# An encoder step: other score banks for the memory steps, input weight splits in parts, memory splits later

## The chip, the cores and the metric

The kernel runs on 1 core of one Trainium2 chip. The metric is the device time of one execution in microseconds (us). Its engines work side by side: TensorE (PE in the profile, with its weight loads as PEld), VectorE (DVE), ScalarE (ACT), GpSimd (POOL) and SyncE (SP), which here only issues transfers. Each runs its own instruction list in order and waits on semaphores that the others raise.

## The reference

One inference step of a one-layer streaming encoder, all in float32: 1024 prompt tokens and 8 x 16 sample tokens (9 tiles of 128 tokens), model width 1024. What matters here, shortened:

```python
qa, ka, va, qb, kb, vb = project(rmsnorm(hp, g_attn), w_in, pos_p)      # 1024 x 2304, rotary on q and k
oa = swa_prompt(qa, ka, va, a_sinks)                # windowed attention with sinks
ob = rmsnorm(diff_prompt(qb, kb, vb, lam), g_subln) * (1.0 - lam_init)  # (softmax1 - lam*softmax2) @ v, 4 heads
hp = hp + jnp.concatenate([oa, ob], axis=-1) @ w_out
mk, mv = mem_kv(mem_prompt, g_mem, w_xkv)           # memory keys and values: 256 x 1024 @ 1024 x 2048
hp = hp + cross_attn(rmsnorm(hp, g_cross), mk, mv, w_xq, w_xo)
hp = hp + sq_relu_mlp(rmsnorm(hp, g_mlp), w_up, w_down)
y_prompt = rmsnorm(hp, g_final)
# the same for the 8 sample streams, against their caches; new keys, values, windows are outputs too
```

## The kernel before

Every float32 product is made from three float32r products: an operand is split into a high part (a copy that rounds, on ScalarE) and a low part (the difference, on VectorE), and TensorE adds high x high, high x low and low x high in a PSUM bank. Weights come in units of 1024 x 256 values, 1 MB each: units 0 to 8 are `w_in`, 9 to 16 `w_xkv`, 17 to 20 `w_out`. A unit is loaded into one of two slots of `w_raw` (`load_next` on ScalarE's queue), `split_hi` copies 128 x 2048 values into `w_hi`, `split_lo` (L1403) subtracts them into `w_lo` in one instruction, L1406. `project` (L1867) makes one projection: 24 matmuls (8 slices of k times 3 products) of 256 columns, for one tile of tokens and one unit. Projections are numbered q. Each is evacuated by VectorE into `stage` (`finish_projection`, L1427; with rotary it is three or four instructions), and GpSimd issues the store.

First stage (to about 60 us): the nine tiles of x are squared (ScalarE), their root is taken (GpSimd), they are scaled (VectorE), transposed on TensorE (`turn`, L1845, 8 transposes a tile) and split (`turned_hi`, `turned_lo`), and unit 0 is projected. TensorE turns tile t + 1 ahead of projection t. VectorE's order for tile t is: scale tile t + 2, low part of tile t + 1, evacuate projection t. GpSimd takes the store of projection t - 2 before the root of tile t + 1.

Then units 1 and 2, and from 115 us on the attention, a software pipeline over the 84 entries of `STEPS`, of which steps 0 to 63 are one phase: steps 0 to 15 are heads 0 and 1 of the differential attention ("diff", t = 0 to 7 key tiles), 16 to 39 the windowed one ("swa", and "swas" for samples), 40 to 63 heads 2 and 3 with the eight samples ("diffs") between them. In step i TensorE issues: scores of i, a preparing transpose (`PREP`: keys, queries, head tiles, memory tiles), value product of i - 2, other transposes, a projection "beside" (`BESIDE`), transposes of the probabilities of i - 1. VectorE in step i: output copy of i - 3 (`out_dve`), maxima of i (`row_max`), sums and combination of i - 1 (`combine`), the low parts of prepared tiles, then `finish_beside` for the step's projections, each followed by `split_lo` of the next unit when q is the first of its unit. ScalarE in step i: transposed probabilities of i - 2, exponentials of i, copies of prepared tiles, and at a unit's first projection `unit_begun`: load of unit u + 2 and `split_hi` of unit u + 1.

`KV_BESIDE` lists, counted from step 40, the 16 steps that get a projection of the memory. PSUM has 8 banks: scores use 0 to 3, transposed probabilities 4 and 5, outputs 6, and bank 7 is shared by nearly all preparing transposes and, in steps 40 to 65, by all memory projections (`beside_bank`, L157). A projection on bank 7 waits for the copy of the last prepared tile there and a preparing transpose waits for the evacuation of the last projection. Scores of a "diff" step with t < 4 in heads 2 and 3 use two banks of one parity, with t >= 4 all four, those of "diffs" banks 0 and 1. Windowed scores use banks 0 and 1 in every step, so each waits for the exponentials of the step before.

The last memory projection is in step 65. When it has ended, SyncE loads three tiles of the residual, and the output projection, the cross attention and the MLP follow from about 632 us on.

## Time and profile before

| | us |
|---|---|
| three runs: median (lowest to highest) | 1876.59 (1875.58 to 1884.19) |
| the profiled execution | 1878.05 |
| its span, first to last instruction | 1876.2 |
| TensorE busy | 1757.1 (94%) |
| VectorE busy | 879.5 (47%) |
| ScalarE busy | 545.9 (29%) |
| GpSimd busy | 172.2 (9%) |

The chain of work that ended last is 84% TensorE, 6% VectorE, 3% ScalarE, 3% transfers. Times below are counted from the start of the span. In a timeline a row is start, duration, engine, line, operation, output <- inputs, shapes, count and, in brackets, how long the engine had idled and what ended that. TensorE's times depend on the clock that was granted; it has two levels, 1.2 and 2.4 GHz, and a granted clock of 1.00 is the upper one.

### The profile page before, as it was taken

Reading aid. Unit: us, or ns where it says so; the run is one execution under the profiler, and the core shown is the slowest. Engines: PE = TensorE matmul, PEld = TensorE weight load, DVE = VectorE, ACT = ScalarE, POOL = GpSimd, SP = SyncE. Lnnn points to the kernel's source line nnn. Section 1 sums busy time; section 2 is a strip of 40 time slices with the busy share of each in tenths; the row PEclk is TensorE's granted clock in tenths of the full one; section 3 lists DMA queues with packets and bytes.
Section 4 is the critical chain, followed back from the end, with each engine's and each line's share of the span. In section 5 each row is a group of like instructions: output and inputs, shape, how many; then the busy total and the mean of one; then the engine's idle time right before and its main releaser. Section 6 shows DMA issues by size and latency. Waiting matters only on the chain.

```text
span 1876.2 us, 29420 instructions
## 1 busy us (share of the span) xinstructions
PE 1757.1 (94%) x11905; PEld 1623.3 (87%) x11905; DVE 879.5 (47%) x1683; ACT 545.9 (29%) x1192; POOL 172.2 (9%) x355
## 2 busy tenths in 40 slices
PE   5998989987797799998999999999999999999997
PEld 5998889876676799997889999999999999999996
DVE  4557555655445425323432554444444444444445
ACT  4213343565444214104520421111111111111112
POOL 2113321112112101110000100000000000000002
PEclk9999999989998899999999999999999999999998
DMA  6312322245453620726451011111111111101102
GB/s 206 108 63 65 105 65 81 66 148 162 165 183 111 240 75 16 263 96 231 171 180 46 23 47 44 45 45 45 45 45 45 45 45 45 36 31 45 56 0 101
DMA packets 107484, 170.39 MB, mean 91 GB/s; under 512 B 7497, under 2 KB 75721, under 8 KB 107369
## 3 DMA queue, kind: packets, MB, share of 16 engines
q1 hardware_dynamic: 79464, 126.78, 20.0%
q0 software_dynamic: 8160, 22.29, 3.5%
q10 hardware_dynamic: 19760, 19.92, 3.3%
q8 instruction: 71, 1.16, 0.3%
q14 instruction: 29, 0.23, 0.0%
HBM read 138.17 MB, written 31.72 MB: 91 GB/s over the span
## 4 chain that ended last, share of the span: by engine, by line
PE 84%; DVE 6%; DMA 3%; ACT 3%; issue 3%; POOL 1%; SPq 0%; ACTq 0%; DVEq 0%; POOLq 0%
PE banks L1922 27%; PE banks L1875 24%; PE banks L2303 21%; PE banks L2012 2%; DMA w_raw<-in_cache_mem_k 1%; DVE w_lo L1406 1%; PE banks L2069 1%; PE banks L1863 1%; PE banks L2171 1%; PE banks L2191 1%; PE banks L2160 1%; PE banks L2099 1%; PE banks L2139 1%; ACT probs L1236 1%; PE banks L2049 1%
## 5 line engine op out<-in xcount | busy, mean ns | idle before, releaser
L1875 PE MATMUL banks<-w_hi,xt_hi 128*128 128x256 f32 x1224 | 355.3, 290 | 13.6 <-DVE xt_lo L1420 3.0
L1875 PE MATMUL banks<-w_lo,xt_hi 128*128 128x256 f32 x1224 | 344.5, 281 | 0.0
L1875 PE MATMUL banks<-w_hi,xt_lo 128*128 128x256 f32 x1224 | 344.4, 281 | 0.0
L1922 PE MATMUL banks<-xt_hi,w_hi 128*128 128x384 f32 x960 | 323.0, 336 | 0.0
L1922 PE MATMUL banks<-xt_hi,w_lo 128*128 128x384 f32 x960 | 322.7, 336 | 0.0
L1922 PE MATMUL banks<-xt_lo,w_hi 128*128 128x384 f32 x960 | 322.6, 336 | 0.0
L1875 PEld LDWEIGHTS banks<-w_hi,xt_hi 128*128 128x128 f32 x1224 | 233.1, 190 | 21.4 <-issue 9.2
L1070 ACT ACTIVATE w_hi<-w_raw 128x2048 fp32r<-128x2048 f32 x61 | 116.8, 1916 | 418.9 <-PE banks L2303 225.8
L1799 DVE TENSOR_TENSOR h<-h,banks 128x512 f32<-128x512 f32 x288 | 192.2, 685 | 98.7 <-PE banks L2303 96.7
L1875 PEld LDWEIGHTS banks<-w_lo,xt_hi 128*128 128x128 f32 x1224 | 233.2, 191 | 0.0
L1875 PEld LDWEIGHTS banks<-w_hi,xt_lo 128*128 128x128 f32 x1224 | 232.9, 190 | 0.0
L2303 PE MATMUL banks<-w_hi,hid_hi 128*128 128x512 f32 x576 | 224.9, 390 | 0.0
L2303 PE MATMUL banks<-w_hi,hid_lo 128*128 128x512 f32 x576 | 224.6, 390 | 0.0
L2303 PE MATMUL banks<-w_lo,hid_hi 128*128 128x512 f32 x576 | 224.0, 389 | 0.0
L1779 DVE TENSOR_TENSOR sq<-sq 128x384 f32<-128x384 f32 x96 | 49.3, 555 | 305.9 <-ACT hid_hi L1355 305.9
L1922 PEld LDWEIGHTS banks<-xt_lo,w_hi 128*128 128x128 f32 x960 | 180.5, 188 | 1.4
L1922 PEld LDWEIGHTS banks<-xt_hi,w_hi 128*128 128x128 f32 x960 | 180.5, 188 | 1.2
L1922 PEld LDWEIGHTS banks<-xt_hi,w_lo 128*128 128x128 f32 x960 | 180.5, 188 | 0.0
L1352 ACT ACTIVATE sq<-banks 128x384 f32<-128x384 f32 x96 | 47.1, 492 | 389.8 <-PE banks L1922 389.7
L2303 PEld LDWEIGHTS banks<-w_hi,hid_lo 128*128 128x128 f32 x576 | 108.1, 188 | 23.4
L2303 PEld LDWEIGHTS banks<-w_lo,hid_hi 128*128 128x128 f32 x576 | 108.1, 188 | 21.5
L2303 PEld LDWEIGHTS banks<-w_hi,hid_hi 128*128 128x128 f32 x576 | 108.1, 188 | 21.2
(217 smaller groups left out, 2231.4 us busy)
## 6 DMA issues: line engine op xcount, KB each, us to landing
w_raw<-in_w_up SPq DMA_DIRECT2D x16, 1024.0 KB, 5.3
w_raw<-in_w_down SPq DMA_DIRECT2D x16, 1024.0 KB, 4.9
w_raw<-in_w_xkv ACTq DMA_DIRECT2D x8, 1024.0 KB, 7.1
kc_diff<-in_cache_diff_k SPq DMA_DIRECT2D x16, 512.0 KB, 3.9
vc_diff<-in_cache_diff_v SPq DMA_DIRECT2D x8, 1024.0 KB, 5.9
w_raw<-in_cache_mem_k SPq DMA_DIRECT2D x16, 512.0 KB, 8.0
w_raw<-in_w_in ACTq DMA_DIRECT2D x7, 1024.0 KB, 5.7
scaled<-mix_d SPq DMA_DIRECT2D x9, 512.0 KB, 5.6
```

The source lines that it names most:

```text
L1070: return nc.scalar.activation(out, in_, ACT.Copy, **kw)
L1236: last = nc.scalar.activation(p[:, g, :], s[:, g, :], ACT.Exp, bias=bias, accum_out=den[:, i % 4, c:c + 1])
L1352: nc.scalar.activation(sq[:, parity, b, :], ps[2 * parity + b][:, 0:CH], ACT.Relu).then_inc(s_relu, 1)
L1406: V.tensor_tensor(w_lo[:, wslot(u), :], w_raw[:, u % 2, :], w_hi[:, wslot(u), :].bitcast(F32), ALU.subtract).then_inc(s_wlo, 1)
L1779: V.tensor_tensor(sq[:, parity, b, :], sq[:, parity, b, :], sq[:, parity, b, :], ALU.mult)\
L1799: V.tensor_tensor(dst, dst, ps[4 + (6 * (3 * odd + c) + d) % 4], ALU.add).then_inc(s_hadd, 1)
L1863: last = tr(ps[4 + (n + 2) % 4][:, k * P:(k + 1) * P], scaled[:, f % 2, blk * P:(blk + 1) * P], ident[:, :])
L1875: last = mm(out, xt[:, k, tok:tok + P], w[:, k, :], start=(k == 0 and n == 0), stop=(k == KD - 1 and n == 2))
L1922: last = mm(out, w[:, k, :], xt[:, k, tok:tok + CH], start=(k == 0 and n == 0), stop=(k == KD - 1 and n == 2))
L2012: last = tr(ps[b][:, g * P:(g + 1) * P], blk, ident[:, :])
L2049: last = mm(score_parts(i, v)[:, g, P * (first - x + 1):NMEM], qt_swa[rows, x % 2, 2 * y + g, :], kt_swa[rows, first * P:(x + 1) * P], sta ...
L2303: last = mm(out, x[:, parity, b, rows], w[:, b, cs], start=(b == 0 and n == 0), stop=(b == GF - 1 and n == 2))
```

## The change

1. `KV_BESIDE`: memory projections leave steps 47 and 49 (7 and 9 in the list) and go to steps 60 and 62 (20 and 22).
2. `beside_bank`: in steps 40 to 63 they use bank 2 in "diffs" steps, bank 3 or 2 (the one that the scores' parity leaves free) in "diff" steps with t < 4, and bank 7 only with t >= 4. The waits between projections and preparing transposes are kept for each bank (`projected`, `prepped`).
3. Splits: units 4 to 9 are split in four parts of 512 columns, the high parts 0 and 1 in the step in which the unit before begins, 2 and 3 one step later; the low parts one step after each. Units 10 to 18 stay whole, their high part where it was, their low part one step later. In VectorE's step the low parts now come before the step's evacuations.
4. `score_bank`: windowed steps from 35 on alternate between banks 0, 1 and 2, 3.
5. In the first stage TensorE makes projection 0 before it turns tile 1.

```diff
@@ -147,7 +147,7 @@
 
-KV_BESIDE = [I_D2 + _i for _i in (5, 7, 8, 9, 10, 12, 13, 14, 16, 17, 18, 19, 21, 23, 24, 25)]
+KV_BESIDE = [I_D2 + _i for _i in (5, 8, 10, 12, 13, 14, 16, 17, 18, 19, 20, 21, 22, 23, 24, 25)]
 BESIDE = _dealt()
@@ -161,6 +161,10 @@
         return 2 + q % 2
+    if i < I_X and STEPS[i][0] == "diffs":
+        return 2
+    if i < I_X and STEPS[i][2] < 4:
+        return 3 - i % 2
     return 7
@@ -354,6 +358,7 @@
         s_whi = sem("s_whi")
+        s_whp = sem("s_whp")
         s_wlo = sem("s_wlo")
@@ -488,6 +493,18 @@
 
+        SPLIT_0 = 4
+        HI_AT, LO_AT = {i: [] for i in range(I_X + 4)}, {i: [] for i in range(I_X + 4)}
+        for u in range(SPLIT_0 - 1, U_OUT + 1):
+            begun = BESIDE_AT[first_step(u)] if u < U_OUT else I_KV_DONE
+            if u < U_KV:
+                for half in range(2):
+                    HI_AT[begun + half].append((u + 1, (2 * half, 2 * half + 1)))
+                    LO_AT[begun + 1 + half].append((u + 1, (2 * half, 2 * half + 1)))
+            else:
+                HI_AT[begun].append((u + 1, None))
+                LO_AT[begun + 1].append((u + 1, None))
+
         def bank_of(q):
@@ -586,7 +603,7 @@
             if kind == "swa":
-                return j
+                return 2 * (i % 2) + j if i > I_IN_DONE else j
             if kind == "swas":
@@ -1114,7 +1131,18 @@
                     load_next(u + 2)
-                split_hi(u + 1)
+
+            def split_hi_parts(u, parts):
+
+                if parts is None:
+                    split_hi(u)
+                    return
+                for c in parts:
+                    if c == 0:
+                        act.wait_ge(s_raw[u % 2], 16 * (u // 2 + 1))
+                        act.wait_ge(s_gemm, last_step(u - 2) + 1)
+                    cs = slice(512 * c, 512 * c + 512)
+                    copy(w_hi[:, wslot(u), cs], w_raw[:, u % 2, cs]).then_inc(s_whi if c == 3 else s_whp, 1)
 
@@ -1131,6 +1159,7 @@
                     unit_begun(UNIT_AT[q])
+                    split_hi(UNIT_AT[q] + 1)
                 roped_hi(q - 2)
@@ -1294,6 +1323,9 @@
                         unit_begun(U_OUT)
+                    if first == 0:
+                        for u, parts in HI_AT[i]:
+                            split_hi_parts(u, parts)
 
@@ -1303,6 +1335,7 @@
             unit_begun(U_OUT + 1)
+            split_hi(U_OUT + 2)
             split_hi(U_OUT + 3)
@@ -1421,6 +1454,22 @@
                                     ALU.subtract).then_inc(s_xt, 1)
+
+            def split_lo_parts(u, parts):
+
+                if parts is None:
+                    split_lo(u)
+                    return
+                for c in parts:
+                    if c == 3:
+                        dve.wait_ge(s_whi, u + 1)
+                    else:
+                        dve.wait_ge(s_whp, 3 * (u - SPLIT_0) + c + 1)
+                    cs = slice(512 * c, 512 * c + 512)
+                    last = V.tensor_tensor(w_lo[:, wslot(u), cs], w_raw[:, u % 2, cs], w_hi[:, wslot(u), cs].bitcast(F32),
+                                           ALU.subtract)
+                    if c == 3:
+                        last.then_inc(s_wlo, 1)
 
@@ -1492,7 +1541,7 @@
                 finish_projection(q)
-                if q in UNIT_AT:
+                if q in UNIT_AT and q < Q_BESIDE:
                     split_lo(UNIT_AT[q] + 1)
@@ -1700,10 +1749,11 @@
                         scale_mem()
-                    for q in BESIDE.get(i, ()) if first == 0 else ():
-                        finish_beside(q)
-                    if first == 0 and i == I_KV_DONE:
-                        split_lo(U_OUT + 1)
+                    if first == 0:
+                        for u, parts in LO_AT[i]:
+                            split_lo_parts(u, parts)
+                        for q in BESIDE.get(i, ()):
+                            finish_beside(q)
                     if first <= i - 2 < end and STEPS[i - 2][0] == "crosss":
@@ -1890,10 +1940,9 @@
                         pe.wait_ge(s_exp, scored)
-                    if beside_bank(q) == 7 and preps_done:
-                        pe.wait_ge(*prepared(preps_done[-1]))
-                    if beside_bank(q) == 7:
-                        on_bank_7.append(q)
+                    if beside_bank(q) in prepped:
+                        pe.wait_ge(*prepared(prepped[beside_bank(q)]))
+                    projected[beside_bank(q)] = q
                 if q < Q_KV:
@@ -1923,16 +1972,18 @@
 
-            preps_done, on_bank_7 = [], []
+            prepped, projected = {}, {}
 
             pe.wait_ge(s_ident, 16)
             turn(0)
             pe.wait_ge(s_wlo, 1)
             for t in range(TT):
-                if t + 1 < TT:
+                if 1 <= t < TT - 1:
                     turn(t + 1)
                 pe.wait_ge(s_xt, 2 * (t + 1))
                 project(Q_IN + t, 0, xt_hi, xt_lo, t * P)
+                if t == 0:
+                    turn(1)
             def turn_roped(q):
@@ -1958,12 +2009,11 @@
                     pe.wait_ge(*prepared(before))
-                if b == 7 and on_bank_7:
-                    pe.wait_ge(s_evac, on_bank_7[-1] + 1)
+                if b in projected and PREP_LIST[n][0] in range(I_X):
+                    pe.wait_ge(s_evac, projected[b] + 1)
                 if b < 4 and PREP_LIST[n][0] in range(I_D2, I_X):
                     pe.wait_ge(s_exp, halves_on(b, PREP_LIST[n][0]))
-                if b == 7:
-                    preps_done.append(n)
+                prepped[b] = n
                 count = 4
```

## Rows read from the trace of the kernel before

**Rows 1.** Page, clock digits of TensorE: 40 slices, tenths of full clock.

```profile
PEclk9999999989998899999999999999999999999998
```

**Rows 2.** Busy windows: us, PE, PEld, DVE, ACT, POOL busy (x), PEclk, DMA, GB/s.

```profile
388.00:421.80 33.80, 25.31 (x180) 21.78 (x176) 17.64 (x61) 21.77 (x76) 5.11 (x7) 0.85 0.57 187
421.80:454.20 32.40, 23.30 (x198) 18.08 (x198) 16.63 (x48) 19.35 (x55) 6.20 (x13) 0.89 0.45 136
...
571.00:622.90 51.90, 39.14 (x287) 35.34 (x287) 25.66 (x55) 21.29 (x56) 11.81 (x26) 0.80 0.21 68
```

**Rows 3.** TensorE's waits, 421.8 to 622.9 us: total us, times, longest.

```profile
PE banks L1875 <- ACT ktc_diff L1070: 6.9, 4, 2.9
PE banks L2171 <- DVE mix L1616: 6.2, 3, 2.6
...
PE banks L2069 <- ACT probs L1236: 3.4, 4, 1.1
```

**Rows 4.** Timeline of steps 62, 64 and 65.

```profile
586.82 2.47 PE L2171 MATMUL banks<-head_v,turned 128*128 128x128 f32 x10 [2.58 <-DVE mix L1616]
...
611.70 2.28 DVE L1406 TENSOR_TENSOR w_lo<-w_raw,w_hi 128x2048 fp32r<-128x2048 f32 x1
...
616.43 3.55 PE L2171 MATMUL banks<-head_v,turned 128*128 128x128 f32 x16 [4.24 <-DVE ostage L1606]
```

**Rows 5.** Busy windows of steps 47, 49, 60, 62; then timeline of 47.

```profile
465.82:477.63 11.81, 8.90 (x89) 7.74 (x89) 4.01 (x10) 3.54 (x9) 0.61 (x1) 0.86 0.50 169
484.28:495.34 11.06, 7.95 (x67) 7.08 (x67) 6.04 (x12) 4.45 (x10) 2.11 (x6) 1.00 0.43 150
571.03:576.23 5.20, 3.66 (x32) 3.06 (x31) 3.01 (x10) 3.04 (x9) 2.09 (x5) 1.00 0.11 39
582.75:591.98 9.23, 5.50 (x28) 4.50 (x29) 6.41 (x10) 5.02 (x10) 1.38 (x4) 0.67 0.35 121
...
471.83 0.59 ACT L1070 ACTIVATE ktc_diff<-banks 128x512 f32<-128x512 f32 x1
472.56 0.35 PE L1875 MATMUL banks<-w_hi,xm_hi 128*128 128x256 f32 x1 [2.91 <-ACT ktc_diff L1070]
```

**Rows 6.** Timeline, tiles 0 to 2: start, us, engine, line, operation, [idle <- releaser].

```profile
17.69 1.28 DVE L1420 TENSOR_TENSOR xt_lo<-banks,xt_hi 128x512 fp32r<-128x512 f32 x2
17.92 1.94 PE L1863 MATMUL banks<-ident,scaled 128*128 128x128 f32 x8 [7.40 <-DVE scaled L1413]
...
19.51 0.56 PE L1875 MATMUL banks<-w_hi,xt_hi 128*128 128x256 f32 x1
...
23.87 1.03 PE L1863 MATMUL banks<-ident,scaled 128*128 128x128 f32 x8
24.07 0.42 DVE L1439 COPY stage<-banks 128x256 f32<-128x256 f32 x1 [2.70 <-PE banks L1875]
24.50 1.09 ACT L1070 ACTIVATE xt_hi<-banks 128x512 fp32r<-128x512 f32 x2 [2.97 <-PE banks L1863]
...
26.51 1.29 DVE L1413 SCALAR_TENSOR_TENSOR scaled<-x_in,rstd,gain 128x1024 f32<-128x1024 f32 x1 [2.02 <-POOL rstd L967]
```

**Rows 7.** VectorE's groups by form: count, busy us, mean ns, idle before.

```profile
L1420 DVE TENSOR_TENSOR xt_lo<-banks,xt_hi 128x512 fp32r<-128x512 f32 x72 | 46.1, 685 | 30.1 <-ACT xt_hi L1070 26.6 <-DMA h<-in_x_prompt 3.4
```

**Rows 8.** Timeline, TensorE, value product of step 19.

```profile
291.78 1.40 PE L2160 MATMUL banks<-v_swa,turned 128*128 128x64 f32 x8 [1.72 <-issue]
```

**Rows 9.** Timeline, TensorE, second projections of steps 4 and 5.

```profile
156.27 0.38 PE L1875 MATMUL banks<-w_hi,xt_hi 128*128 128x256 f32 x1 [1.75 <-DVE stage L1456]
...
166.05 0.39 PE L1875 MATMUL banks<-w_hi,xt_hi 128*128 128x256 f32 x1 [1.10 <-DVE stage L1456]
```

**Rows 10.** Timeline, TensorE, steps 36 and 38.

```profile
397.00 1.09 PE L2012 MATMUL banks<-ident,q_raw 128*128 128x128 f32 x4 [2.57 <-DMA q_raw<-q_swa_d]
...
409.65 1.14 PE L2049 MATMUL banks<-kt_swa,qt_swa 64*128 64x256 f32 x8 [1.35 <-ACT esink L1241]
```

**Rows 11.** DMA issues, 440 to 625 us: count, KB, median to landing.

```profile
w_raw<-in_w_xkv ACTq DMA_DIRECT2D x6, 1024.0 KB, 7.4
```
## Prediction

> **What bounds the kernel now.** I read the page first: TensorE is busy for 94% of the span, and its clock digits dip in the first slice and from about 390 to 660 us, the ninth to the fourteenth [rows 1]. The stretches by window say which part of that the change can reach: from 388 to 421.8 us TensorE works 25.3 of 33.8 us, from 421.8 to 454.2 us 23.3 of 32.4 us, and from 571 to 622.9 us 39.1 of 51.9 us at a granted clock of 0.80 [rows 2]. Outside these it has little to give. So the order of TensorE's own instructions and what each of its waits ends on set the time here; VectorE and ScalarE matter only where they hold it. Then the waits of 421.8 to 622.9 us: projections wait 6.9 us in 4 places for a ScalarE copy out of the shared bank 7, and value products wait 6.2 us in 3 places for a small VectorE copy that is queued behind a 2.28 us weight subtraction [rows 3, 4]. I number the attention steps 0 to 63 by their place in `STEPS`; step 47 begins at 465.8 us and step 62 at 582.8 us [rows 5].
>
> The profiled execution took 1878.05 us with a span of 1876.2 us; the three runs have the median 1876.59 us. The sum below is made against 1878.05 us, and the median lies 1.5 us under it.
>
> **The change, part by part.** Minus is a gain.
>
> *First nine tiles.* Before, the transposes of tile 1 start at 17.92 us and hold the first projection, whose operands VectorE finishes at 17.69 + 1.28 = 18.97 us, until 19.51 us [rows 6]. The change lets the projection go first: 0.5 us earlier. But on VectorE the low part of tile 1 stands ahead of the evacuation of projection 0, and it now waits for transposes that come behind that projection. That projection takes from 19.51 to about 23.8 us, mostly at the low clock (a later one takes 3.05 us), so it would end near 23.5 us; ScalarE's copies follow 0.63 us after the transposes begin (24.50 after 23.87), VectorE's subtraction some 0.7 us later and takes 1.28 us, so the evacuation starts at about 26.1 us where it was 24.07 us [rows 6]. From there the old ring runs: evacuation, the store that GpSimd issues, GpSimd's root, VectorE's scaling 2.44 us later (26.51), which again gates the next tile [rows 6]. TensorE has slack in this ring and VectorE with GpSimd has none, so the delay is carried to the end of the stage: +2.0 us. If the transposes still run at the low clock (1.94 instead of 1.03 us) and the projection too, it is +3.5 us; below that I see no more than -0.5 us, if the ring had slack. I take +2.0.
>
> *Input splits in four parts over two steps.* Six units (4 to 9) change from one 2.28 us piece on VectorE, after an evacuation, to two halves ahead of an evacuation, one and two steps later. One 512-column subtraction is 685 ns, two together 1.28 us [rows 7], so four are 0.69 + 3 x 0.60 = 2.5 us, 0.2 us over the whole piece. The Trainium skill (VectorE: DVE Perf Modes, the errata section) says that such instructions pay a fixed extra cost each, and its formula gives 691 ns for 512 and 2291 ns for 2048 columns; by it four parts would be 0.47 us dearer a split, against this edit, where overlapping neighbours in the trace give half of that. Where the split stood between a ScalarE copy and a value product it stopped TensorE: 1.72 us at 291.78 us [rows 8], and 2.18 us in a second such place at 337.45 us. Both go, and a projection at 292.9 us that a clock dip lengthened by about 1 us may go with them: -4.3 us, of which the halves give back up to 0.5 us. At steps 4 and 5 two projections share bank 7 and the second waits for the first's evacuation, 1.75 us with a split ahead of the step and 1.10 us without [rows 9]. A half now stands ahead of each of these two evacuations: about +0.3 and +1.1 us. The other three units fall beside projections that alternate on banks: nothing, and up to +1.1 us each if not. Together -2.9 us (between -4.5 and 0).
>
> *Score banks of the last windowed steps.* For steps 35 to 39 the score banks alternate. Step 36's early scores gain nothing, since the transpose behind them waits for a transfer until 397.00 us [rows 10]. The scores of steps 38 and 39 no longer wait for the exponentials of the step before, 1.35 us and 1.16 us (the latter in the same view at 415.15 us) [rows 10]. Behind them the loop through VectorE's maxima, four exponentials and the sum remains, and it starts about 1.1 us earlier a step: -2.2 us (0 to -3.5; nothing if that loop alone bounds them).
>
> *Memory splits one step later, ahead of the evacuation.* These eight splits stay whole. They leave the end of a step, where the next step's small copies queued behind them, and lie while TensorE runs a 3.05 us projection. The three waits of 6.2 us are steps 57, 59 and 62 (1.5, 2.1 and 2.6 us) [rows 3]. At 611.70 us a split of 2.28 us precedes the copy on which the last value product waits 4.24 us [rows 4]; the rest of that wait, eight small scalings, stays. Steps 46, 51 and 53 show three more of the same kind, 0.8, 0.4 and 0.4 us. Without step 62, which I count below: -1.5 - 2.1 - 2.3 - 1.6 = -7.5 us. What becomes late next is the scores' wait for the exponentials, so I keep 0 to -9 us.
>
> *Bank 2 or 3 instead of 7, and two projections moved.* Steps 47 and 49 lose their projection, 60 and 62 get one. Step 47 is 11.8 us long at a clock of 0.86: its projection waits 2.91 us for the copy of 471.83 us out of bank 7 and starts at 472.56 us [rows 5]. Without it the next scores need that same copy (their keys) and can start about 472.5 us, 6.7 us after the step's start: -5.1 us. Step 49, 11.1 us [rows 5], has the same shape; its split is gone as well, the second copy is done some 6.6 us after its start: -4.4 us. Steps 50 and 52 lose their waits on bank 7, 0.8 and 0.3 us of the 6.9 us [rows 3]. Step 60 (5.2 us, TensorE busy 3.7 us [rows 5]) takes a 3.05 us projection: 1.25 + 1.1 + 3.05 + 1.3 = 6.6 us, +1.4 us. Step 62 (9.2 us at clock 0.67, TensorE waiting 2.58 us for a copy behind a split [rows 4, 5]) becomes 1.7 + 1.2 + 3.05 + 0.8 = 6.8 us at the full clock, -2.4 us. Step 63, whose scores now take 1.66 instead of 2.93 us, -1.3 us. Sum -11.9 us (-6 if the dips stay and the scores wait elsewhere, -14).
>
> *Costs and gains not in the trace of before.* Scores that now share bank 2 or 3 with the projection just before must wait for its evacuation, 0.43 us under a 0.3 to 1.2 us transpose: +0.1 us in ten places, +1 us (0 to +3). Steps 46, 47, 49 and 51 are left without a projection. Steps 40 to 44, which have none either, ran at a clock of 0.89 [rows 2]; I add one short dip, about +2 us (0 to +5). In steps 64 and 65 the projections and value products of 604 to 623 us ran partly at the low clock (3.55 us for the last product of 16 short matmuls [rows 4], in a stretch whose clock is 0.80 [rows 2]); with less idling before them a part comes back, -1.5 us (0 to -4).
>
> All behind 622.9 us hangs on the last memory projection: its end releases the residual loads, so the gain is carried on whole. Sum: +2.0 - 2.9 - 2.2 - 7.5 - 11.9 + 1.0 + 2.0 - 1.5 = -21.0 us, giving 1857.0 us for the profiled execution and 1855.5 us for the median. I forecast 1855.5 us.
>
> **The rivals.** *The cover is thin at the end (20%).* Units now begin every second step from 56 to 64. Each needs a 1 MB weight load, whose issue is on ScalarE; those loads took 7.4 us in the median from 440 to 625 us [rows 11]. Two steps are 13 to 14 us, so there is cover; but if the exponentials and the split on ScalarE then wait on the load, or the subtraction outlasts the projection beside it, steps 57 to 65 keep their old length. That takes away 1.5 + 2.1 + 2.4 + 1.3 + 1.5 us, about 9 us: 1864.5 us.
>
> *The clock gives way (7%), ending slower.* The projections are what keeps TensorE dense in steps 46 to 52. If this stretch of about 60 us ran wholly at the low clock, the steps would be bound by TensorE: step 47 4.7 x 2 = 9.4 us against 6.7 (+2.7), step 49 10.8 against 6.6 (+4.2), steps 48 and 50 +6.7 and +7.1, and 51 and 52 about +6 together: +27 us, ending at 1882.5 us. It becomes slower than before when more than 0.8 of the stretch is at the low clock. Against it: steps 40 to 44 kept 0.89, and 388 to 421.8 us 0.85 [rows 2]. The Trainium skill (TensorE: Matmul & The Clock Gate, on oscillation in real kernels) says that a wait between every two bursts of matmuls can put the array back to the lower clock each time; by that rule this rival is what happens, and rows 2 bear it out only for a part of each stretch.
>
> *The change doesn't reach the chain (6%).* If the steps from 40 on are paced by the loop of scores, maxima, exponentials and sum, as 3.4 us of score waits on exponentials hint [rows 3], banks and splits only move waits. What is left is steps 47 and 49 without their clock part, -8 us, the last split, -2.3 us, less 3.05 x 2 us of projections and +2.0 us at the start: about -2 us, 1874.5 us.
>
> **How the numbers follow.** Forecast as reasoned 67%: 1855.5 us, itself between 1848 and 1861 us by the bounds. The three rivals 20, 7 and 6%. The range is 1846 to 1868 us: it takes in the first rival and leaves out the two others and the ends. A measurement of this kernel tells 0.5% from no change, that is below 1867.2 us or above 1886.0 us. Faster: 0.67 + 0.20 and a little less for its tail, 0.85. Within: the two last rivals mostly, 0.11. Slower: 0.04, the clock rival with a longer stretch.
>
> **What would show it.** The evacuation of projection 0 at about 26.1 us, and the end of the nine tiles 2 us later; no 1.7 and 2.2 us waits near 290 and 335 us, but longer waits for evacuations at steps 4 and 5; no wait of a memory projection on a key copy; steps 47 and 49 under 7 us; no value product waiting on a copy behind a subtraction; a clock above 0.9 in the last 50 us before the output projection, and that end some 21 us earlier. Wrong it would be if the clock digits between 440 and 600 us fall, or if ScalarE waits on weight loads there.

## The result and the profile after

The changed kernel takes 1852.77 us (median of four runs, 1851.67 to 1854.58), the kernel before beside it 1879.91 us (four runs, 1875.58 to 1884.19): a ratio of 0.986 with a 95% interval of 0.984 to 0.987. The forecast was 1855.5 us, in a range of 1846 to 1868 us. The profiled executions are 1878.05 us before and 1852.38 us after, 25.7 us apart where the sum said 21.0 us. The page of the changed kernel, its span and its clock digits:

```profile
span 1850.0 us, 29463 instructions
...
PEclk9999999988999899999999999999999999999998
```

Against [rows 1] the tenth digit (416 to 463 us) fell from 9 to 8 and the thirteenth rose from 8 to 9; slices of 46 us are too coarse. Windows that are cut at the steps tell it. First before, then after: the span from the first tile to step 0, steps 0 to 39, steps 40 to 64, and the rest (us, then busy us and count of PE, PEld, DVE, ACT, POOL; granted clock; DMA share; GB/s).

```profile
17.00:115.50 98.50, 92.58 (x744) 90.42 (x744) 56.65 (x115) 26.93 (x48) 16.04 (x31) 0.98 0.31 96
115.50:421.90 306.40, 278.63 (x2255) 257.81 (x2255) 185.07 (x554) 132.16 (x411) 73.05 (x140) 0.98 0.29 91
421.90:616.40 194.50, 154.96 (x1444) 130.62 (x1445) 98.38 (x220) 96.07 (x231) 35.83 (x81) 0.91 0.47 154
616.40:1876.00 1259.60, 1228.98 (x7456) 1142.84 (x7456) 535.39 (x795) 283.32 (x493) 44.90 (x93) 0.99 0.22 78
```

```profile
17.00:117.80 100.80, 91.75 (x744) 88.67 (x744) 56.70 (x115) 26.56 (x48) 16.06 (x31) 1.00 0.30 93
117.80:419.90 302.10, 278.95 (x2253) 258.08 (x2253) 185.70 (x572) 132.94 (x429) 74.60 (x140) 0.98 0.29 92
419.90:591.60 171.70, 148.46 (x1445) 126.53 (x1445) 96.30 (x219) 95.65 (x231) 42.98 (x81) 0.94 0.54 175
591.60:1850.00 1258.40, 1226.10 (x7456) 1140.14 (x7456) 537.31 (x796) 282.89 (x493) 44.70 (x93) 0.99 0.22 78
```

So +2.3, -4.3, -22.8 and -1.2 us. The third pair is the one to read closely: the same matmuls (1444 and 1445 records) took 155.0 us and take 148.5 us, at a clock of 0.91 and 0.94. That is 6.5 us from the clock. TensorE's idle time went from 194.5 - 155.0 = 39.5 us to 171.7 - 148.5 = 23.2 us, which is 16.3 us from waits. I use this cut, busy time of the same instructions against idle time, for every run below.

The clock did not rise everywhere in it. Steps 40 to 46, before and after:

```profile
421.86:465.82 43.96, 33.18 (x288) 26.38 (x288) 23.38 (x59) 26.10 (x69) 9.23 (x21) 0.92 0.53 166
```

```profile
419.94:465.86 45.92, 37.18 (x286) 30.00 (x287) 22.34 (x58) 26.18 (x69) 9.68 (x20) 0.81 0.50 158
```

TensorE waits 2.0 us less there, but the same matmuls take 4.0 us more at the lower clock, so this stretch became 2 us longer. All of the gain lies behind it.

The four steps of [rows 5], after (steps 47, 49, 60, 62, same columns):

```profile
465.90:472.50 6.60, 4.55 (x65) 3.30 (x65) 5.27 (x14) 3.53 (x10) 2.10 (x3) 1.00 0.37 112
479.20:485.60 6.40, 4.92 (x45) 4.39 (x44) 4.01 (x13) 4.50 (x11) 2.21 (x6) 1.00 0.31 84
552.30:558.40 6.10, 6.10 (x54) 5.85 (x54) 3.19 (x10) 3.89 (x8) 2.27 (x6) 1.00 0.52 163
564.90:571.70 6.80, 6.33 (x52) 5.79 (x53) 5.73 (x12) 3.35 (x9) 1.81 (x5) 1.00 0.09 28
```

Steps 47 and 49 went from 11.8 and 11.1 us to 6.7 and 6.4 us, and step 60 is now wholly TensorE: 6.10 us busy of 6.1 us.

TensorE's waits in the stretch of [rows 3], and three rows of its timeline (start, duration, then in brackets the idle time before and what ended it):

```profile
PE banks L2140 <- ACT ktc_diff L1087: 6.6, 5, 1.9
PE banks L2221 <- ACT turned L1087: 3.2, 1, 3.2
PE banks L2221 <- DVE ostage L1655: 2.0, 1, 2.0
...
PE banks L2119 <- ACT probs L1265: 1.3, 2, 0.9
```

```profile
472.53 1.06 PE L2140 MATMUL banks<-ktc_diff,zd 128*32 128x512 f32 x8 [1.85 <-ACT ktc_diff L1087]
485.59 1.06 PE L2140 MATMUL banks<-ktc_diff,zd 128*32 128x512 f32 x8 [1.48 <-ACT ktc_diff L1087]
...
591.56 2.02 PE L2221 MATMUL banks<-head_v,turned 128*128 128x128 f32 x16 [2.03 <-DVE ostage L1655]
```

No projection waits for a key copy any more and no value product for `mix`, which were 6.9 and 6.2 us in [rows 3]. The key copy has not lost its importance: the next scores (L2140) wait for it instead, 6.6 us in five places. But they wait in a step that is shorter by a whole projection. The last value product waits 2.03 us where it waited 4.24 us [rows 4].

In the first stage, tiles 0 to 2 (the first matmul of projection 0, its transposes after it, then ScalarE's copy, VectorE's low part, the evacuation, and the scalings that follow):

```profile
19.19 0.55 PE L1925 MATMUL banks<-w_hi,xt_hi 128*128 128x256 f32 x1 [8.65 <-DVE xt_lo L1453]
...
24.09 1.91 PE L1913 MATMUL banks<-ident,scaled 128*128 128x128 f32 x16
24.73 1.08 ACT L1087 ACTIVATE xt_hi<-banks 128x512 fp32r<-128x512 f32 x2 [8.40 <-PE banks L1913]
25.36 1.29 DVE L1453 TENSOR_TENSOR xt_lo<-banks,xt_hi 128x512 fp32r<-128x512 f32 x2 [5.12 <-ACT xt_hi L1087]
26.56 0.41 DVE L1488 COPY stage<-banks 128x256 f32<-128x256 f32 x1
...
28.99 1.29 DVE L1446 SCALAR_TENSOR_TENSOR scaled<-x_in,rstd,gain 128x1024 f32<-128x1024 f32 x1 [2.01 <-POOL rstd L984]
33.67 1.28 DVE L1446 SCALAR_TENSOR_TENSOR scaled<-x_in,rstd,gain 128x1024 f32<-128x1024 f32 x1 [1.87 <-POOL rstd L984]
```

The projection starts 0.3 us earlier than in [rows 6] and the evacuation 2.5 us later (26.56 against 24.07). The scaling behind it comes at 28.99 us instead of 26.51 us, and five scalings later (54.51 against 52.05 us) nothing has been made up. The 1.91 us are those of 16 transposes, tiles 1 and 2 one behind the other.

At steps 4 and 5 the second projections (cf. [rows 9]) wait longer, as the halves now stand ahead of the evacuations:

```profile
158.92 0.39 PE L1925 MATMUL banks<-w_hi,xt_hi 128*128 128x256 f32 x1 [2.08 <-DVE stage L1505]
171.42 0.38 PE L1925 MATMUL banks<-w_hi,xt_hi 128*128 128x256 f32 x1 [2.29 <-DVE stage L1505]
```

### The profile page after: what moved, and what is told of

It is laid out like the page before. It is cut to its first block, busy times and chain, and to the rows that moved or that the text cites. A ratio compares the mean times of both kernels' runs of the same rounds, so it can differ in the third digit from the quotient of the medians.

```text
span 1850.0 us, 29463 instructions
## 1 busy us (share of the span) xinstructions
PE 1747.2 (94%) x11905; PEld 1615.0 (87%) x11905; DVE 879.9 (48%) x1701; ACT 545.4 (29%) x1210; POOL 180.6 (10%) x355
## 3 DMA queue, kind: packets, MB, share of 16 engines
q8 instruction: 71, 1.16, 0.3%
## 4 chain that ended last, share of the span: by engine, by line
PE 87%; DVE 4%; DMA 3%; ACT 3%; issue 2%; POOL 1%; SPq 0%; ACTq 0%; DVEq 0%; POOLq 0%
PE banks L1971 27%; PE banks L1925 24%; PE banks L2353 21%; PE banks L2062 2%; PE banks L2119 2%; PE banks L2241 1%; PE banks L2221 1%; PE banks L2189 1%; PE banks L2149 1%; PE banks L1913 1%; PE banks L2210 1%; DMA w_raw<-in_cache_mem_k 1%; ACT probs L1265 1%; PE banks L2099 1%; DVE xt_lo L1453 1%
## 5 line engine op out<-in xcount | busy, mean ns | idle before, releaser
L1087 ACT ACTIVATE w_hi<-w_raw 128x2048 fp32r<-128x2048 f32 (+1 forms) x79 | 119.1, 1523 | 418.8 <-PE banks L2353 225.8
```

The source lines that it names most:

```text
L1087: return nc.scalar.activation(out, in_, ACT.Copy, **kw)
```

## The experiments

The theory: about 12 us of the gain come from the moved projections (with their banks), 8 us from the later memory splits, 3 us from the input splits and 2 us from the score banks, and the reorder of the first tiles costs 2 us. The main rival: most of it is the clock, or the list only together with the banks. Each edit undoes or adds something against the changed kernel; line numbers of the profile shift by up to 4. Runs are compared with the kernel before on the same chip, and by the length of single steps.

### The old order of the first tiles

```diff
-                if 1 <= t < TT - 1:
+                if t + 1 < TT:
                     turn(t + 1)
...
-                if t == 0:
-                    turn(1)
```

> The changed kernel with one part undone: TensorE again turns tile 1 before it makes projection 0. Theory (the reorder delays the evacuation of projection 0, and the ring of VectorE and GpSimd carries that on): step 0 begins at 115.5 us as in the kernel before, where the changed kernel has 117.8 us; span 1847.7 us against 1850.0 us (1846.7 to 1849). Rival (the reorder is worth 0.5 us by the earlier start, and the 2.3 us come from elsewhere): step 0 at 117.8 to 118.3 us, span 1850 to 1850.5 us.

> Tile 1 turned before projection 0 (the kernel of the first experiment), now timed beside the changed kernel. Its single time there was 8.1 us below the changed kernel's, of which its trace puts 2.6 us to the first stage and the rest to steps that ran with fewer clock dips. Theory (the dips fall by chance of timing from run to run, the reorder costs 2.3 to 2.6 us): median 2 to 4 us below the changed kernel's, the single times spread over 4 us or more. Rival (the shift makes the dips rarer in every run): 6 to 9 us below.

> The changed kernel itself, timed beside the two others. Theory: 1851 to 1856 us, with a spread of several us from where clock dips fall; ratio to the kernel before 0.984 to 0.988. Rival to the forecast's sum (most of the gain was a lucky placing of dips in one trace): a ratio of 0.99 or more.

Step 0 begins at 115.2 us, 2.6 us earlier, as the ring theory says. But the single run took 1844.29 us, 8 us less than the changed kernel. Where the other 5 us were is told by the windows of steps 40 to 64, first of this run and then of a later run of the same kernel:

```profile
415.90:581.10 165.20, 140.69 (x1445) 120.47 (x1445) 96.05 (x219) 95.21 (x231) 42.99 (x81) 0.99 0.55 181
```

```profile
418.90:589.50 170.60, 148.00 (x1445) 125.64 (x1445) 96.13 (x219) 95.69 (x231) 43.10 (x81) 0.94 0.54 176
```

The idle time is 24.5 and 22.6 us, so no better in the first; its busy time is 7.3 us shorter, at a clock of 0.99. That was not the edit. Timed side by side on one chip, in five runs each, the old order gives 1851.26 us (ratio 0.984, 0.982 to 0.985) and the changed kernel 1853.61 us (0.985, 0.983 to 0.986): 2.35 us apart, with step 0 at 116.0 and 118.2 us. The intervals of the two ratios overlap, so it is the place of step 0 that shows the 2.3 to 2.6 us, and the medians agree with it. The five times of each kernel spread over 3.5 and 4.4 us.

### The GpSimd store one tile later

```diff
-                if t >= 2:
-                    store(Q_IN + t - 2)
-            for q in range(Q_IN + TT - 2, Q_BESIDE):
+                if t >= 3:
+                    store(Q_IN + t - 3)
+            for q in range(Q_IN + TT - 3, Q_BESIDE):
```

> The changed kernel with the order of its first tiles, but GpSimd issues the store of a projection one tile later, so that the root of the next tile no longer waits for an evacuation. Theory (a ring of evacuation, store, root and scaling paces the first stage at 4.66 us a tile): the ring opens, TensorE's 3.05 + 1.04 us a tile becomes the bound, and step 0 begins 3 to 5 us earlier than the 117.8 us of the changed kernel; the projections lie about 4.1 us apart. Rival (TensorE's own order or ScalarE's squares pace it): step 0 within 0.7 us of 117.8 us.

It took 1844.35 us in a single run, and step 0 begins at 110.9 us instead of 117.8 us. VectorE's scalings here, against those of the changed kernel above:

```profile
28.64 1.28 DVE L1446 SCALAR_TENSOR_TENSOR scaled<-x_in,rstd,gain 128x1024 f32<-128x1024 f32 x1 [0.82 <-POOL rstd L984]
31.38 1.27 DVE L1446 SCALAR_TENSOR_TENSOR scaled<-x_in,rstd,gain 128x1024 f32<-128x1024 f32 x1
36.51 1.28 DVE L1446 SCALAR_TENSOR_TENSOR scaled<-x_in,rstd,gain 128x1024 f32<-128x1024 f32 x1
```

With the store ahead of the root, each scaling waits 1.9 us for GpSimd, and the tile takes 33.67 - 28.99 = 4.68 us. With the root ahead, only the first one waits. So evacuation, store, root and scaling do form the ring, and it is what carries the reorder's delay. I had expected 3 to 5 us and 4.1 us from projection to projection; it is 6.9 us, and the later evacuations come 3.7 us apart, as the root no longer hangs on the evacuation at all.

### The input splits whole and in their old place

```diff
-                for half in range(2):
-                    HI_AT[begun + half].append((u + 1, (2 * half, 2 * half + 1)))
-                    LO_AT[begun + 1 + half].append((u + 1, (2 * half, 2 * half + 1)))
+                HI_AT[begun].append((u + 1, None))
...
-                if q in UNIT_AT and q < Q_BESIDE:
+                if q in UNIT_AT and q < Q_KV:
```

> The changed kernel with units 4 to 9 split whole and in the old place; memory splits, banks and order as changed. Theory, from the step lengths of both traces: steps 4 and 5 get 3.0 us shorter, steps 19 and 27 get 3.5 and 2.2 us longer, steps 9 and 29 cancel, so the span is about 1852.5 us (1850.5 to 1854.5): the splits in parts pay for two units and cost for one. Rival (the parts only move waits, and the shorter steps 19 and 27 come from something else): span 1847 to 1850.5 us, steps 19 and 27 stay at 5.8 and 4.6 us.

1857.57 us in a single run, 5 us above the changed kernel. The rows that belong to the edit are back as they were before:

```profile
159.29 0.39 PE L1923 MATMUL banks<-w_hi,xt_hi 128*128 128x256 f32 x1 [1.79 <-DVE stage L1503]
169.04 0.38 PE L1923 MATMUL banks<-w_hi,xt_hi 128*128 128x256 f32 x1 [1.10 <-DVE stage L1503]
...
294.84 1.08 PE L2208 MATMUL banks<-v_swa,turned 128*128 128x64 f32 x8 [1.74 <-issue]
```

Steps 4 and 5 last 10.1 and 9.9 us (12.0 and 11.1 us changed), steps 19 and 27 last 7.7 and 8.75 us (5.75 and 4.6 us). So the splitting costs at steps 4 and 5 and pays at 19 and 27, as told. In step 27 a fall of the clock adds 1.9 us to the 2.2 us wait; with it the span of 1855.8 us is 1.3 us above my range. Steps 4 and 5 have at least one too, 1.5 us each, in eight of the ten traces in which both halves stand ahead of the evacuations, and in none of the three others (before, this one and the last experiment). So part of what the splitting costs comes through the clock.

### The last windowed steps on the old score banks

```diff
-                return 2 * (i % 2) + j if i > I_IN_DONE else j
+                return j
```

> The changed kernel with the windowed scores of steps 35 to 39 on banks 0 and 1 in every step again. Theory: waits for exponentials of 1.1 to 1.4 us come back at steps 38 and 39, step 40 begins 2.0 to 2.5 us later than in the changed kernel (counted from step 34), the span 1852 to 1852.5 us. Rival (the loop of maxima and exponentials bounds them anyway): step 40 at most 0.5 us later, span 1850 us.

1856.08 us in a single run. Step 40 begins at 422.2 us instead of 419.9 us, with step 34 at the same place within 0.1 us: 2.3 us. The scores of steps 36, 38 and 39 wait 1.74, 1.07 and 1.16 us for the exponentials again, as in the kernel before (1.75, 1.35 and 1.16 us). The span, 1854.2 us, is 1.7 us above what I expected; the step's place is what shows the edit.

### Projections: banks and places apart

The old bank 7 and the old list together:

```diff
-KV_BESIDE = [I_D2 + _i for _i in (5, 8, 10, 12, 13, 14, 16, 17, 18, 19, 20, 21, 22, 23, 24, 25)]
+KV_BESIDE = [I_D2 + _i for _i in (5, 7, 8, 9, 10, 12, 13, 14, 16, 17, 18, 19, 21, 23, 24, 25)]
...
-    if i < I_X and STEPS[i][0] == "diffs":
-        return 2
-    if i < I_X and STEPS[i][2] < 4:
-        return 3 - i % 2
```

> The changed kernel with the old list of steps for memory projections and all of them on bank 7 again; memory splits stay one step later. Theory (the moved projections are the largest part): step 47 back to about 11.8 us and step 49 to 9 to 10 us, steps 60 and 62 at 5.2 and 6 us or less, the span 8 to 14 us longer, near 1861 us. Rival (the gain of the memory steps comes from the splits that moved, and projections only change place, 24 matmuls for 24 matmuls): span at most 4 us longer, up to 1854 us.

Only the list undone (first part of that diff):

> The changed kernel with the old list of steps for memory projections, on the new banks (steps 47 and 49 have t of 4 and more, so they stay on bank 7). Theory (the two moved projections carry the gain, the other banks about 1.1 us): about like the kernel with old banks and old list, span 1866 to 1870 us, step 47 and 49 at 11 to 13 us, steps 50 and 52 shorter by 0.8 and 0.3 us. Rival (the other banks carry it): span 1850 to 1856 us.

Only the banks undone (second part):

> The changed kernel with all memory projections on bank 7 again, in the new steps. Theory: waits for copies out of bank 7 come back at steps 50 and 52 (0.8 and 0.3 us) and small ones at 48, 53, 54, 57, 58; span 1851 to 1854 us where clock dips fall as in the changed kernel. Rival (the banks carry it): span 1858 us or more.

Both undone: 1868.87 us (four runs, 1864.68 to 1872.39, ratio 0.993, 0.991 to 0.995), 15 to 16 us more than the changed kernel's 1853.61 and 1852.77 us elsewhere, where 8 to 14 us were expected. Only the list undone: 1861.03 us, only the banks undone: 1856.58 us, a single run each. The spans of these two, 1859.1 and 1854.7 us, lie below the theory's 1866 to 1870 us and just above its 1851 to 1854 us; the first lies outside the rival's range too. Steps 40 to 64 in the three (order: both, list, banks):

```profile
421.60:610.50 188.90, 160.38 (x1445) 136.22 (x1445) 96.28 (x219) 96.18 (x231) 46.98 (x81) 0.87 0.48 159
```

```profile
421.40:600.20 178.80, 149.41 (x1445) 128.24 (x1445) 96.24 (x219) 95.79 (x231) 46.24 (x81) 0.93 0.51 168
```

```profile
420.90:596.00 175.10, 151.23 (x1444) 128.29 (x1444) 96.19 (x219) 95.70 (x231) 43.10 (x81) 0.92 0.52 171
```

Idle time is 28.5, 29.4 and 23.9 us, against 23.2 us. So the list is worth 6.2 us of waits by itself, and the banks 0.7 us with the new list. With the old list they take 1.1 us of waits from steps 50 and 52 too, but step 64 then waits 3.56 us instead of 1.98 us, and nothing is left. Busy time is 160.4, 149.4 and 151.2 us against 148.5 us: the rest is the clock, and it differs by 11 us between two kernels whose waits are nearly the same. The place of the list's waits, here step 47, old list with old banks and old list with new banks:

```profile
473.89 0.55 PE L1921 MATMUL banks<-w_hi,xm_hi 128*128 128x256 f32 x1 [2.94 <-ACT ktc_diff L1083]
```

```profile
472.19 0.36 PE L1925 MATMUL banks<-w_hi,xm_hi 128*128 128x256 f32 x1 [2.92 <-ACT ktc_diff L1087]
```

The new banks take nothing from this wait, nor from that of step 49 (2.65 and 2.60 us): in steps 47 and 49 (t of 4 or more) the projection is on bank 7 under either rule. What the banks do is in steps 50 and 52, 8.6 and 12.0 us with bank 7 against 7.6 and 9.95 us without, of which 0.8 and 0.3 us are waits and most of the rest in step 52 is the clock (0.87 there against 1.00).

### The memory weights' low part back in its place

```diff
-                LO_AT[begun + 1].append((u + 1, None))
...
-                if q in UNIT_AT and q < Q_BESIDE:
+                if q in UNIT_AT and (q < Q_BESIDE or q >= Q_KV):
...
+                        if i == I_KV_DONE:
+                            split_lo(U_OUT + 1)
```

> The changed kernel with the low parts of units 10 to 18 back in the old place, after the evacuation of the unit's first projection and in its own step; banks and list as changed. Theory (a 2.28 us subtraction ahead of the small copies holds value products): waits of 1.5 to 2.6 us for a VectorE copy come back at four to six steps from 51 to 62, and 2.3 us before the last value product; the span 6 to 11 us longer, near 1859 us. Rival (with the projections moved, the steps are bound by the loop of scores, maxima and exponentials, and the splits are hidden in either place): at most 3 us longer, up to 1853 us.

1866.14 us (four runs, 1861.45 to 1871.35, ratio 0.991, 0.989 to 0.993), some 13 us more than the changed kernel, where 6 to 11 us were expected. Its waits from step 57 on, and steps 40 to 64:

```profile
PE banks L2222 <- DVE ostage L1654: 6.2, 2, 4.2
PE banks L2222 <- DVE mix L1664: 3.6, 2, 2.1
```

```profile
420.30:608.20 187.90, 155.51 (x1444) 131.55 (x1445) 98.86 (x220) 96.12 (x231) 36.18 (x81) 0.91 0.49 159
```

The waits of [rows 3, 4] are back to the number (1.49 and 2.09 us in steps 57 and 59, 4.24 us before the last product), and steps 61 and 63 show some of 1.8 and 1.9 us that the kernel before did not have there, since units begin in steps 60 and 62 under the new list and not in 61. Idle time is 32.4 us, 9.2 us more; busy time is 7.1 us more.

### All that the runs pointed to, together

```diff
-                    LO_AT[begun + 1 + half].append((u + 1, (2 * half, 2 * half + 1)))
+                    LO_AT[begun + (3 if u == 4 else 1) + half].append((u + 1, (2 * half, 2 * half + 1)))
...
-            load_head_queries_keys(2)
             load_band_queries(8)
+            load_head_queries_keys(2)
+            load_head_values(2, s_head_in)
             sp.dma_start(q8, q_diff_d[SEQ:TOK, :]).then_inc(s_q8, 16)
             sp.dma_start(k8, dk_s).then_inc(s_q8, 16)
-            load_head_values(2, s_head_in)
...
-                if 1 <= t < TT - 1:
+                if t + 1 < TT:
                     turn(t + 1)
```

To this come the later store, and in the last attention steps the eight samples' small squares (ScalarE, to behind the transposed probabilities) and scalings (VectorE, to the end of the step).

> The changed kernel with six things on top that the traces point to: tile 1 turned before projection 0; the stores of the first stage one tile later; the low parts of unit 5 at steps 6 and 7, where no second projection of the step waits for an evacuation; SyncE issues the last windowed queries ahead of the head tiles; the eight squares and eight scalings of the sample outputs behind the copies that value products wait for. Theory: step 0 begins near 109 us (-8.5), steps 4 and 5 are 10.2 and 9.9 us (-3), step 36 loses most of its 2.6 us wait for a transfer and perhaps the clock dip behind it, though step 37 then waits for head tiles (-3 to -7), the last two value products wait 2.4 and 2.0 us less (-4.4). Together -19 to -23 us against the changed kernel, 1830 to 1834 us. Rival (waits only move to the next loop from step 4 on): the first stage's gain alone, 1843 to 1846 us.

1827.01 us (five runs, 1825.1 to 1830.24, ratio 0.971, 0.970 to 0.972), 26.6 us less than the changed kernel on the same chip, and less than the 1830 to 1834 us that I expected. By the traces of the two: step 0 begins 10.4 us earlier (107.8 against 118.2 us), steps 4 and 5 are 3.9 us shorter, steps 36 and 37 6.6 us, steps 40 to 64 2.9 us, and the rest 3.2 us. These sum to 27.0 us; the spans are 26.8 us apart, of which 10.3 us is TensorE's busy time and so mostly the clock. In steps 4 and 5 the clock is 1.6 of the 3.9 us. The last two products wait 2.8 us less, where 4.4 us were expected. The transfer order is the surprise among them. Step 36's transposes, first after and then here:

```profile
396.75 1.08 PE L2062 MATMUL banks<-ident,q_raw 128*128 128x128 f32 x4 [3.65 <-DMA q_raw<-q_swa_d]
```

```profile
379.16 0.63 PE L2060 MATMUL banks<-ident,q_raw 128*128 128x128 f32 x4
...
385.01 0.63 PE L2060 MATMUL banks<-ident,head_raw 128*128 128x128 f32 x4 [0.58 <-DMA head_v<-out_diff_v_prompt]
```

The query tile's transfer was behind two head tiles in SyncE's list. Ahead of them, step 36 lasts 5.4 us instead of 10.8 us. Of that, 2.9 us are waits and 2.6 us the clock, which is 1.00 in steps 36 and 37 here. As six edits were made at once, only the rows tell them apart, and none of the six but the old tile order and the later store was run by itself.

## Why the prediction was right

**Right, by its main step.** The bound was read rightly: TensorE's own order and the ends of its waits, in the stretch behind 390 us. Each of the five parts carried the sign that was given to it, and undoing each on its own brought back its own rows, the banks' being the smallest (0.7 us of waits with the new list). The single undoings add up to some 34 us and the whole gain is 27 us, so the parts are not independent, and the steps' own lengths are the better measure. What was measured, part by part, against the terms:

*First nine tiles, +2.0.* It is +2.3 us at step 0, and 2.3 to 2.6 us when undone. The evacuation was forecast at 26.1 us and came at 26.56 us. The projection made the difference: its matmuls start 0.21 us apart until 23.6 us and 0.12 us apart from there, so that it ended at 24.09 us and not at 23.5 us. The transposes ran at the full rate (16 in 1.91 us, where 8 took 1.03 us in [rows 6]), so the +3.5 us case did not come.

*Input splits, -2.9.* Steps 4, 5, 9, 19, 27 and 29 changed by +1.8, +1.2, -0.5, -3.5, -2.2 and +0.7 us, together -2.5 us. The inner terms were less good than their sum. The second projections of steps 4 and 5 wait 2.08 and 2.29 us, +0.3 and +1.2 us as forecast, but a fall of the clock made step 4 1.5 us longer. In a second trace of the same kernel step 4 lasts 10.4 us with the same wait, and step 5 has the fall and lasts 12.6 us, so the sum is the same 23 us. The forecast of -4.3 us for steps 19 and 27 was 1.4 us short, because the fall of the clock in step 19 went wholly, and one unit was not free (step 29). The 24 pieces of 512 columns take a mean of 684 ns, and 15.4 us together, which is 2.6 us for each four (2.5 us told):

```profile
L1469 DVE TENSOR_TENSOR w_lo<-w_raw,w_hi 128x512 fp32r<-128x512 f32 x24 | 15.4, 684 | 0.0
```

*Score banks, -2.2.* Steps 34 to 39 changed by -1.9 us together, and 2.3 us return with the old banks. Step 36's early scores gained nothing, as told: their wait of 1.75 us went and that for the transfer grew from 2.57 to 3.65 us.

*Memory splits, -7.5.* Steps 46, 54, 57 and 59 gained 1.2, 0.5, 1.7 and 1.9 us, and the last product's wait 2.2 us, together 7.5 us. Undone, 9.2 us of idle time come back. The rest of the last product's wait (2.03 us) did stay, as told.

*Moved projections and banks, -11.9.* Steps 47 and 49: -5.1 and -4.7 us, where -5.1 and -4.4 us were told. The next scores start at 472.53 us less 465.9 us = 6.6 us into the step, waiting for the key copy (6.7 us told). Step 60 +0.95 us (+1.4 told), step 62 -2.4 us (-2.4), step 63 -1.3 us (-1.3). Step 50 -1.1 us (-0.8 told). Step 52 is 2.0 us shorter where -0.3 us was told, but that is mostly the clock, and is counted below. Without it these steps gained 14.0 us. The prediction's own terms, -5.1 - 4.4 - 0.8 - 0.3 + 1.4 - 2.4 - 1.3, add up to -12.9 us and not to the -11.9 us that it wrote and carried into its sum.

**Mis-sized terms.** The span fell by 26.2 us where the sum said 21.0 us, or 22.0 us when it is added rightly. By the starts of the steps:

| | told, us | measured, us |
|---|---|---|
| first nine tiles | +2.0 | +2.3 |
| input splits | -2.9 | -2.5 |
| score banks | -2.2 | -1.9 |
| memory splits | -7.5 | -7.5 |
| moved projections and banks | -12.9 (written -11.9) | -14.0 |
| added costs: one dip of the clock, evacuation waits | +3.0 | +3.2 (steps 40 to 45) |
| clock from step 64 on, without the last wait | -1.5 | -2.5 |
| rest of steps 51 and 52 | none | -3.4 |

The dip came, though not where it was told. Steps 46 to 51, for which it was told, ran at the full clock. In steps 40 to 45, which have the same matmuls as before, the low clock cost 4.4 us and 1.2 us less waiting gave a part back. The waits for evacuations are 0.17 to 0.24 us in three places (steps 46, 60 and 62), about 0.6 us together and not 1 us in ten. The term that was missed is the clock in steps 51 and 52: at 0.83 and 0.85 before, at 1.00 after. Before, then after:

```profile
504.00:514.20 10.20, 7.56 (x52) 6.25 (x55) 7.99 (x14) 5.53 (x11) 2.09 (x5) 0.83 0.46 149
514.20:526.10 11.90, 10.14 (x108) 7.65 (x103) 2.71 (x5) 3.74 (x9) 0.07 (x1) 0.85 0.49 175
```

```profile
493.10:501.50 8.40, 5.96 (x50) 4.89 (x49) 6.48 (x12) 5.42 (x11) 3.28 (x4) 1.00 0.64 219
501.50:511.40 9.90, 8.41 (x107) 6.89 (x106) 4.14 (x8) 3.69 (x9) 0.61 (x1) 1.00 0.65 224
```

That is 1.8 us and 2.0 us, of which 3.3 us are busy time and 0.5 us waits (0.3 us of it told for step 52). That the forecast of 1855.5 us lies only 2.7 us off has a part of luck: it started from 1876.59 us, and with its fourth run the kernel before has a median of 1879.91 us, so the gain is 27.1 us, 6.1 us more than told.

**The rivals.** The cover at the end was not thin: steps 57 to 65 became shorter together, and neither TensorE nor ScalarE waits for a weight load there. The change reached the chain. Over the whole span TensorE's busy time fell by 9.9 us (1757.1 to 1747.2 us) and its idle time by 16.3 us, so the clock is over a third of the gain and not most of it. The clock did not give way as a whole: from step 40 to 64 it rose from 0.91 to 0.94, with two steps at 1.00 that have no projection now. But it did fall from 0.92 to 0.81 in steps 40 to 46, and the tenth digit fell with it, which the prediction had named as a sign of being wrong (digits between 440 and 600 us). The sign was too coarse for what it was to show, as the steps that lost projections are not the ones that slowed down. The Trainium skill (TensorE: Matmul & The Clock Gate, "HAM oscillation — how this bites in real kernels") describes matmul bursts with a wait between every two, after each of which the array was back at the lower clock. The runs show falls, but few: with 23 us idle in 172 us, the mean clock was 0.94, and 0.99 in the first run of the old tile order, which has the same steps. So the page's rule names something that happens here, and is no measure of how much of it.

**What stays open.** The two undone kernels (old banks with old list, and old split place) lost 12 and 7 us of busy time beside their 5 and 9 us of waits. The traces speak against chance: in steps 46 to 62 the clock is 0.98 to 1.00 in all eight traces that have the memory steps of the changed kernel, and 0.92 and 0.95 in these two (0.94 before). Each of the two traces is of the slowest of its kernel's four runs, though, so the medians, 15 and 13 us above the changed kernel, are the better measure, and they too are above the 12 and 8 us that the sum gives. Open is the rule behind it: with only the list undone, and nearly the same waits as with list and banks undone, that clock is 0.99. Why steps 40 to 45 run slower in all changed kernels but one trace (0.77 to 0.87, once 0.95, against 0.91 before) is not shown either.

## What to carry to other kernels

Where an engine is at the end of most waits, follow each small copy to what is queued ahead of it. A 2.28 us subtraction, a GpSimd store and two 512 KB transfers each held work that was short and urgent, and moving them behind it gave 9, 7 and 5 us here (the last one with its part of the clock, and made together with five other edits). Put work that fills TensorE where TensorE is idle for another reason, not where it makes the next scores' inputs late: a projection moved from a step that waited for its copy gave 5 us there and cost 1 us in step 60, where TensorE had been idle. And compare kernels by the starts of single steps and by busy and idle time of the same instructions: one span did not tell a 2.4 us edit from an 8 us one.

## What the runs showed of the hardware

The same instructions with the same waits have two lengths. Step 48, in the changed kernel and in the later run of the old tile order, lasts 6.7 and 8.3 us with the same 1.85 us wait ahead of its scores:

```profile
472.50:479.20 6.70, 6.67 (x64) 5.88 (x65) 2.27 (x4) 2.85 (x9) 0.93 (x3) 1.00 0.77 274
```

```profile
470.40:478.70 8.30, 8.29 (x64) 7.26 (x65) 2.25 (x4) 3.00 (x9) 0.94 (x3) 0.79 0.64 217
```

The granted clock was 1.00 in one and 0.79 in the other, that is partly at 1.2 GHz. Step 4 does the same (10.4 and 12.0 us), as do steps 5, 41 and 64. One kernel's spans were 1841.9 us in one execution and 1851.2 us in another, on another chip: its busy time differs by 9.9 us (mean clock 0.989 and 0.984), its idle time by under 1 us. I had thought of the dips as fixed to the places where the profile of before shows them; a forecast that takes one away, as I did for steps 19 and 62, prices a chance and not a certainty.

Some falls do come back at one place, behind one wait. In steps 36 and 37, where TensorE waits 2.6 to 4.0 us for the query tile, the clock is 0.69 to 0.78 in twelve of the thirteen traces; in the thirteenth, that of the last experiment, this wait is gone and the clock is 1.00.
